# Forgetting attention: half a gate unit ahead of the last pair's scores, another half between its two turns

## The reference

```python
qg = xn @ b_w_qg[j]
q = rmsnorm(qg[..., :d].reshape(bsz, s_len, N_HEADS, HEAD_DIM), q_norm[j])
o = forgetting_attention(q, k, v, c)      # per head: softmax(q k^T * scale + c_i - c_j, causal) v
o = o * jax.nn.sigmoid(qg[..., d:])       # the gate
x = x + o @ b_w_out[j]                    # the output projection
```

## Time and profile before

| what | value |
|---|---|
| median of the runs | 2083.39 us |
| lowest and highest run | 2083.32, 2083.63 us |
| span of the profiled execution | 2081.4 us |
| median of the runs less that span | 1.99 us |
| TensorE (PE) busy | 2074.3 us, 100% |
| POOL busy | 1515.7 us, 73% |
| VectorE (DVE) busy | 969.0 us, 47% |
| ScalarE (ACT) busy | 499.3 us, 24% |
| share of the chain of work that ended last | PE 97%, DVE 2%, ACT 1% |

### The profile page before, as it was taken

One profiled execution on the slowest core, in us unless ns is written; L12 is line 12 of the kernel. 1 busy time (PEld: TensorE's weight loads), 2 busy tenths in 40 slices (PEclk: granted clock), 3 DMA queues, 4 the chain that ended last, 5 costly groups with the idle time before them and its releaser, 6 DMA issues.

```text
span 2081.4 us, 28663 instructions
## 1 busy us (share of the span) xinstructions
PE 2074.3 (100%) x10112; PEld 1731.8 (83%) x10112; DVE 969.0 (47%) x1459; ACT 499.3 (24%) x999; POOL 1515.7 (73%) x1607
## 2 busy tenths in 40 slices
PE   9999999999999999999999999999999999999999
PEld 8888888888788878888888888889888888888887
DVE  6566655521456675655542166436753243222100
ACT  2002111100267673211100054222353122111000
POOL 7888888867865547888877775546545788777675
PEclk9999999999999999999999999999999999999999
DMA  5333333323333223333323332223222333333233
GB/s 158 101 89 102 95 101 91 101 84 93 106 108 86 82 82 86 91 101 91 100 86 94 100 90 81 62 71 102 72 68 69 87 110 93 99 93 101 86 91 96
DMA packets 368163, 192.45 MB, mean 92 GB/s; under 512 B 8672, under 2 KB 364608, under 8 KB 368080
## 3 DMA queue, kind: packets, MB, share of 16 engines
q1 hardware_dynamic: 365280, 186.52, 31.2%
q10 hardware_dynamic: 2800, 4.83, 0.7%
HBM read 189.19 MB, written 2.13 MB: 92 GB/s over the span
## 4 chain that ended last, share of the span: by engine, by line
PE 97%; DVE 2%; ACT 1%; DMA 0%; issue 0%; SPq 0%; DVEq 0%; ACTq 0%
PE PS L575 22%; PE PS L577 22%; PE PS L576 22%; PE PS L892 3%; PE PS L894 3%; PE PS L893 3%; PE PS L908 2%; PE PS L909 2%; PE PS L910 2%; PE PS L734 1%; PE PS L735 1%; PE PS L736 1%; PE PS L697 1%; PE PS L1091 1%; PE PS L677 1%; PE PS L762 1%
## 5 line engine op out<-in xcount | busy, mean ns | idle before, releaser
L558 POOL TENSOR_TENSOR RING<-RAW,RING 128x512 fp32r<-128x512 f32 x704 | 976.1, 1386 | 58.7
L555 POOL TENSOR_SCALAR RING<-RAW 128x512 fp32r<-128x512 f32 x704 | 519.6, 738 | 342.9 <-PE PS L894 89.9
L575 PE MATMUL PS<-XH,RING 128*128 128x512 f32 x1296 | 504.8, 389 | 0.0
L576 PE MATMUL PS<-XL,RING 128*128 128x512 f32 x1296 | 504.2, 389 | 0.0
L577 PE MATMUL PS<-XH,RING 128*128 128x512 f32 x1296 | 504.2, 389 | 0.0
L575 PEld LDWEIGHTS PS<-XH,RING 128*128 128x128 f32 x1296 | 243.3, 188 | 51.3 <-issue 1.1
L576 PEld LDWEIGHTS PS<-XL,RING 128*128 128x128 f32 x1296 | 243.3, 188 | 50.6 <-issue 0.2
L577 PEld LDWEIGHTS PS<-XH,RING 128*128 128x128 f32 x1296 | 243.3, 188 | 50.5
L575 PE MATMUL PS<-HH,RING 128*128 128x512 f32 x528 | 205.6, 389 | 0.0
L577 PE MATMUL PS<-HH,RING 128*128 128x512 f32 x528 | 205.4, 389 | 0.0
L576 PE MATMUL PS<-HL,RING 128*128 128x512 f32 x528 | 205.4, 389 | 0.0
(11 more groups left out here) (342 smaller groups left out, 3405.3 us busy)
## 6 DMA issues: line engine op xcount, KB each, us to landing
RAW<-in_ffn_w_up SPq DMA_DIRECT2D x88, 512.0 KB, 3.7
RAW<-in_w_in SPq DMA_DIRECT2D x52, 512.0 KB, 3.7
RAW<-in_w_ffn_in SPq DMA_DIRECT2D x44, 512.0 KB, 3.7
RAW<-in_ffn_w_down SPq DMA_DIRECT2D x32, 512.0 KB, 3.8
RAW<-in_a_w_in SPq DMA_DIRECT2D x24, 512.0 KB, 3.6
RAW<-in_b_w_qg SPq DMA_DIRECT2D x16, 512.0 KB, 3.6
RAW<-in_w_kvf SPq DMA_DIRECT2D x16, 512.0 KB, 3.9
RAW<-in_w_ffn_out SPq DMA_DIRECT2D x16, 512.0 KB, 3.7
```

Of the source, the lines that this page charges most:

```text
L555: hi = pool.tensor_scalar(WH[s][:, k0_:k1, :], RAW[r][:, k0_:k1, :], 1.0, 1.0, ALU.mult, ALU.mult)
L558: lo = pool.tensor_tensor(WL[s][:, k0_:k1, :], RAW[r][:, k0_:k1, :], WH[s][:, k0_:k1, :].bitcast(F32), ALU.subtract)
L575: pe.matmul(o, WH[s][:, k, :], xh[:, k0 + k, :], start=first and k == 0, stop=False)
L576: pe.matmul(o, WH[s][:, k, :], xl[:, k0 + k, :], start=False, stop=False)
```

## The change

The two steps are on TensorE's queue, in the loop over the pairs. The second half of late unit 1 is issued at the end of pair 6, ahead of the scores of pair 7 and of the weighing of pair 6, instead of behind them. And the first half of late unit 3 is issued between the turn of head 0 and the turn of head 1 of pair 7, instead of behind both.

```diff
--- before.py
+++ after.py
@@ -833,11 +833,11 @@
                     if p > 0:
                         weigh(p - 1)
                     if p == PAIRS - 1:
-                        gate_half(1, 1)
                         gate_half(2, 0)
                         gate_half(2, 1)
-                        turn(p)
+                        turn(p, 0)
                         gate_half(3, 0)
+                        turn(p, 1)
                         gate_half(3, 1)
                     elif p % 2 == 0:
                         if p > 0:
@@ -865,6 +865,7 @@
                             head_sums(q_next)
                             turn(p)
                             gate_half(1, 0)
+                            gate_half(1, 1)
                     else:
                         quad = p // 2 + 1
                         value_piece(quad, 0)
```

## The result

The changed kernel takes 2087.11 us (median of 16 runs, 2085.33 to 2088.07), against 2083.51 us for the kernel before in the same session (16 runs, 2083.17 to 2083.92). The ratio is 1.0015, with a 95% interval of 1.0008 to 1.0022: slower by 3.6 us. The forecast was 2086.0, with a range from 2084.0 to 2087.2.

What follows compares the result with a forecast made beforehand. TensorE, at full clock throughout, was taken to bound the kernel. Filled hole -0.84, stall +2.92, extra switch +0.10 gave +2.18 us, +2.6 with the projection's late tail: 2083.4 + 2.6 = 2086.0 us, range 2084.0 to 2087.2.

Steps and rivals of the forecast that it cites:

- The gain: TensorE before pair 7's scores: late unit 1's second half fills the idle hole, reaching the turn 0.84 us earlier.
- The collision: POOL's earlier split takes turns with VectorE's low parts and masks; first pass over pair 7's scores starts 3.09 us later.
- The stall: TensorE before the turn of head 0: waits 2.92 us for the late softmax probabilities.
- The tail: Output projection's first unit: pair 7's result is taken out late, making the shift 2.6 us instead of 2.18.
- The sum without the clock: Whole kernel with TensorE at full clock: +2.6 us, from 2083.4 to 2086.0 us.
- (d): Rival, turn of head 0 and following half unit: stall halves TensorE's clock, another 3.9 us, 2089.9 us; chance 0.04.
- (c): Rival, projection's first unit: main case with a deep tail, +3.5 us in all, 2086.9 us; chance 0.12.
- (a): Rival, pair 7's softmax: POOL's first operation falls behind VectorE's masks, no collision where it matters, 2083.1 us; chance 0.12.
- (b): Rival, pair 7's softmax: masks precede POOL's second subtraction, first pass +2.05, stall 1.9, sum +1.5, 2084.9 us; chance 0.12.
- the cover: Before head 0's turn in the kernel before: its probabilities were ready 1.1 us before TensorE needed them.

Runs made afterwards that it cites:

- e1: Kernel before with only late unit 1's second half ahead of pair 7's scores, both heads turned together: 2086.82 us, ratio 1.0017.
- e3: Changed kernel with POOL's split of output unit 1 held until all passes over pair 7's scores are done: 2082.89 us, ratio 0.9998.
- e4: Changed kernel with VectorE's four low parts of output tiles 0 to 3 moved behind pair 7's softmax: 2082.97 us, ratio 0.9999.
- e2: Kernel before with only late unit 3's first half put between the turns of head 0 and head 1: 2083.72 us, ratio 1.0002.
- e8: Kernel before with seven more ScalarE copies of an unused tile ahead of scaling pair 7's probabilities: 2088.82 us, ratio 1.0026.
- e7: Kernel before with four more ScalarE copies of an unused tile ahead of scaling pair 7's probabilities: 2085.62 us.
- e6: Changed kernel with 12 more TensorE matmuls by a zero weight tile in place of the stall before head 0's turn: 2085.91 us.

## Why the prediction was right, and where it was off

**The gain.** Forecast: scores at 775.04, unit 2 at 779.78, TensorE at the turn at 785.35. Measured 775.10, 779.86 and 785.44, in an execution that came to this place 0.07 us later. Right.

**The collision.** Forecast: split from 775.20, low parts to 779.34, first pass at 780.83. Measured 775.26, 779.35 and 780.81. The turns read off gave the ends of POOL's four operations (776.13, 777.79, 778.82 and 780.49 against 776.04, 777.76, 778.79 and 780.51), of the last low part and of the masks to 0.1 us. e1, e3 and e4 show that it is the cause. The Trainium skill, page "SBUF — State Buffer", section "SBUF: two separate sides", calls this an exclusive lock of the port pair that VectorE and GpSimd (POOL here) share, held for a whole instruction, against a VectorE operation with two SBUF inputs; the trace agrees (4.39 for 2.50 us). Besides, the ends of the instructions fit two engines that take turns when both have work waiting.

**The stall.** Forecast 2.92 us, measured 2.75 (785.44 to 788.19). Of the 0.17 us less, 0.09 is TensorE's later arrival.

**The tail.** Forecast 0.4 us more in the projection's first unit: the matmul that started at 801.17 now starts at 805.12, +3.95, and the projection at 799.92 instead of 796.27, +3.65, so 0.30. The 4.0 us from the last gate to the taking out of pair 7 were 3.97. e2 has the second step alone, at 0.41 us in all.

**The sum without the clock.** Forecast +2.6; the seven runs with full clock have their middle at 2085.66, +2.15. The size was off by 0.45 us. The profiled execution has 3.95 us at the last tile of the first output unit; less the 0.07 it came late and the 1.6 of the clock that is +2.3, so 0.3 of the 0.45 show there, 0.17 as the stall and 0.1 as the tail. The rest lies between this execution and the seven runs, which are themselves 0.6 us apart.

**The clock.** This is the step that was wrong. Case (d) had a chance of 0.04, on the ground that the trace had no stall to judge by; it came in nine of 16 runs and sets the median. And its price was put at 3.9 us, for the turn and the half unit at half clock; measured, the switch and the half unit took 4.42 us (789.26 to 793.68) where 2.83 were forecast, 1.6 us more: eight of the twelve matmuls stood 0.43 us apart instead of 0.227, and the transposes before them had passed at full clock. The case let the lower clock cover all the work from 788.27 to the end of the half unit; in the trace it lasted 3.4 us, from 789.5 on. The page "TensorE: Matmul & The Clock Gate" of the Trainium skill was cited for it, and the trace agrees on the lower level (0.50). That section also remarks that the number of slow matmuls at a kernel's start differs from run to run. Here the same holds behind a stall in the middle of a kernel: by the mean granted clock seven of the 16 runs have none. The median fell 0.09 us inside the range, but the range did not earn that: it was drawn up to 2087.2 for the deep tail of case (c), which did not come. By e1 and the changed kernel (d) deserved a chance of about 0.6, at 1.6 us. With the forecast's own 2086.0 that makes 2087.6, above the measured median by about the 0.45 us by which the sum without the clock was too high. So the median stayed inside the range because the sum was too high by 0.45 us while the clock was left out: that is luck.

**Rivals (a) and (b)** are out: the low parts took 4.39 us, and the masks came behind POOL's second subtraction, at 1.56 us. What (a) describes was built in e3, and cost 2082.89 us, against the 2083.1 that was worked out for it.

## What to carry to other kernels

Before moving work ahead on the engine that bounds, ask what its end releases: here a finished unit freed a ring slot, and POOL's split, 5.7 us earlier, landed on VectorE's instructions ahead of the softmax. Lay the two engines' instructions with two SBUF inputs in turns on paper, since each then ends at a known time, and compare the delay with the cover (here 1.1 us). And where a new stall of TensorE is forecast, give the fall of its clock behind it a real chance and a price (1.6 us here, 0.8 to 2.0 in e8); a trace without such a stall says nothing against it.

## What the runs showed of the hardware

- After 1.3 us of idle time (and 0.5 us more behind the first ten transposes) TensorE's clock fell in 3 of 11 runs (e7), after 2.6 us in 17 of 27 (the changed kernel and e1), after 3.2 us (and 0.5 us more) in 9 of 9 (e8). What decides between two runs of one kernel isn't shown.
- In the three traces with a fall it came 0.1 us (e1), 1.3 us (the changed kernel) and 2.0 us (e8) after work had begun again. The lower level lasted some 3.4 us in each.
- The same late start of the turn with TensorE kept at work (e6) had no fall in 11 runs.
- POOL's instructions and those of VectorE with two SBUF inputs fit turns, one instruction at a time: four of VectorE's and four of POOL's take 5.5 us together (774.96 to 780.49), where VectorE's four alone take 2.5.
